# First input weights of layer 0 queued directly behind x in the same DMA queue

## The reference, cut to what matters

```python
h = x
for layer in range(DEPTH):
    z = rms_norm(h, norm_mix[layer]) @ w_in[layer]        # w_in: 1024 x 2072
    u_ssm, z_conv, q, k_c, v_c, ... = jnp.split(z, cuts, axis=-1)
    y_ssm = s5_mixer(u_ssm, ...)      # complex diagonal scan
    y_conv = conv_mixer(z_conv, ...)  # causal depthwise convolution
    y_nsa = nsa_mixer(q, k_c, ...)    # sparse attention
    h = h + concat(rms of the three) * mix_out_norm @ w_out
    h = h + cross_attention(rms_norm(h), rms_norm(mem), ...)
    h = h + (swiglu if layer is even else top-2-of-8 expert swiglu)(rms_norm(h))
```

## Time and profile before

| what | value |
|---|---|
| median of 3 runs | 1311.87 us (1309.08 to 1317.62) |
| the profiled execution's own time | 1314.63 us |
| span of the profiled execution | 1312.7 us |
| mean granted TensorE clock | 0.993 |
| PE busy | 1259.8 us, 96% of the span |
| DVE busy | 705.5 us, 54% |
| ACT busy | 428.7 us, 33% |
| DMA packets, bytes | 33980, 360.63 MB |

### The profile page before, as it was taken

One profiled execution on the slowest core, in us unless ns is written; L12 is line 12 of the kernel. 1 busy time (PEld: TensorE's weight loads), 2 busy tenths in 40 slices (PEclk: granted clock), 3 DMA queues, 4 the chain that ended last, 5 costly groups with the idle time before them and its releaser, 6 DMA issues.

```text
span 1312.7 us, 49682 instructions
## 1 busy us (share of the span) xinstructions
PE 1259.8 (96%) x21938; PEld 1070.7 (82%) x21938; DVE 705.5 (54%) x1640; ACT 428.7 (33%) x882; POOL 98.4 (7%) x157
## 2 busy tenths in 40 slices
PE   7999998999999999999889999999999999999897
PEld 5756566887887775656589999999999999999896
DVE  7875315647866376531455555555555554554455
ACT  4526313001002132631323333333333333333332
POOL 1360100000000044010000000000000000000010
PEclk9999999999999999999999999999999999999999
DMA  9530025233442543004779999999999999999994
GB/s 371 216 130 1 1 97 207 97 143 147 193 165 92 197 186 129 8 1 192 287 267 427 426 426 426 427 426 424 427 427 426 426 426 427 426 426 427 425 423 191
DMA packets 33980, 360.63 MB, mean 275 GB/s; under 512 B 3875, under 2 KB 5539, under 8 KB 7932
## 3 DMA queue, kind: packets, MB, share of 16 engines
q1 hardware_dynamic: 31184, 354.50, 65.4%
q10 hardware_dynamic: 2156, 3.19, 0.7%
q0 software_dynamic: 576, 2.10, 0.4%
HBM read 356.41 MB, written 3.36 MB: 274 GB/s over the span
## 4 chain that ended last, share of the span: by engine, by line
PE 79%; DMA 9%; DVE 7%; ACT 2%; issue 2%; POOL 0%; ACTq 0%; DVEq 0%; SPq 0%
PE bank L2317 25%; PE bank L1737 24%; PE bank L2334 12%; DMA ring<-moe_w_dram 8%; PE bank L2263 6%; PE bank L1745 2%; PE bank L2304 2%; PE bank L2024 1%; PE bank L1901 1%; PE bank L2111 1%; PE bank L1781 1%; PE bank L2089 1%; PE bank L2353 1%; PE bank L1840 1%; ACT ring L623 0%
## 5 line engine op out<-in xcount | busy, mean ns | idle before, releaser
L2317 PE MATMUL bank<-R,ring 128*64 128x80 f32 x11264 | 430.0, 233 | 15.2 <-DVE ring L1633 10.7
L2317 PEld LDWEIGHTS bank<-R,ring 128*64 128x64 f32 x11264 | 406.4, 137 | 23.7 <-DVE ring L1633 19.1
L1737 PE MATMUL bank<-ring 128*128 128x128 f32 (+2 forms) x1904 | 344.3, 340 | 5.0 <-DVE ring L1054 1.9
L1737 PEld LDWEIGHTS bank<-ring 128*128 128x128 f32 x1904 | 267.6, 192 | 84.9 <-issue 69.3
L899 ACT ACTIVATE ring<-ring 128x1024 f32<-128x1024 f32 x176 | 186.1, 1057 | 149.7 <-PE bank L2334 149.7
L2334 PE MATMUL bank<-zz,ring 128*64 128x80 f32 x5632 | 227.0, 234 | 0.0
L2334 PEld LDWEIGHTS bank<-zz,ring 128*64 128x64 f32 x5632 | 210.1, 138 | 0.0
L1633 DVE COPY ring<-ring 128x1024 f32<-128x1024 f32 x176 | 121.4, 690 | 37.3 <-DMA ring<-moe_w_dram 36.8
L1682 DVE SCALAR_TENSOR_TENSOR zz<-zz,bank 128x80 f32<-128x80 f32 x176 | 41.8, 238 | 158.3 <-PE bank L2317 157.2
L1637 DVE COPY ring<-ring 128x1024 f32<-128x1024 f32 x176 | 120.9, 687 | 0.1
L895 ACT ACTIVATE X<-bank 128x80 f32<-128x80 f32 x176 | 41.7, 237 | 233.5 <-PE bank L2317 232.6
(11 more groups left out here) (328 smaller groups left out, 1119.0 us busy)
## 6 DMA issues: line engine op xcount, KB each, us to landing
ring<-moe_w_dram SPq DMA_DIRECT2D x176, 1536.0 KB, 26.3
ring<-ffn_w_dram SPq DMA_DIRECT2D x11, 3072.0 KB, 10.3
ring<-w_in_dram SPq DMA_DIRECT2D x6, 2048.0 KB, 8.0
ring<-w_out_dram SPq DMA_DIRECT2D x4, 2048.0 KB, 7.8
ring<-w_x_dram SPq DMA_DIRECT2D x2, 3072.0 KB, 10.9
ring<-w_small_dram SPq DMA_DIRECT2D x2, 2896.0 KB, 11.3
ring<-w_in_dram SPq DMA_DIRECT2D x2, 2144.0 KB, 15.4
y_rows_dram<-R SPq DMA_DIRECT2D x7, 320.0 KB, 25.9
```

Of the source, the lines that this page charges most:

```text
L1737: i = pe.matmul(out_ap, a, b, start=(k == 0), stop=(k == n - 1))
L2317: e = pe.matmul(pb[out_bank][c0:c0 + 64, 0:CAP], half[:, P * k + c0:P * k + c0 + 64], xg[:, k], start=(k == 0), stop=(k == KT - 1), tile_p ...
```

## The change

SP no longer waits for x to land before it issues the first chunk of weights. The wait for `t5_loaded` that stands between this chunk and `mem` stays where it is, and no instruction of any other engine is changed. ACT's waits for `x_loaded` stay.

```diff
             for l in range(L):
-                if l == 0:
-                    sp.wait_ge(sem["x_loaded"], 16 * NT)
                 for c in (2, 3, 0, 1) if l else range(4):
                     item(f"in{c}_{l}", w_in[l][:, 4096 * c:4096 * c + (4288 if c == 3 else 4096)])
                     if l == 0 and c == 0:
```

## The result

The changed kernel took 1318.68 us (median of 20 runs, 1314.19 to 1323.64), the kernel before 1314.46 us in 20 runs beside it (1309.08 to 1318.42). The ratio is 1.0032, 95% interval 1.0019 to 1.0044: slower by 4.2 us, 2.5 to 5.8 by the interval.

The account below looks back on a forecast made before the run. The start was taken as bound by the chain from ACT's load of `par` through PE, ACT and DVE. +4.9 (`par`), 0 (weights) and 0 (`mem`) on the median 1311.87 gave 1316.8, said as 1317; range 1311 to 1322.

Parts of the forecast that it names:

- +4.9 us: whole kernel: sum of +4.9 from `par`, 0 for the weights, 0 for `mem`; bounds +4.3 and +4.9.
- The chain starts with `par`, not with the weights: kernel start: PE's work hangs on ACT's load of `par`; PE's 0.84 us wait for `in0_0` is worth nothing.
- One packet of each queue in turn: DMA engines: each takes one packet from q1 and q10 in turn, whatever their sizes, not sharing by bytes.
- The size of the toll, 4.3 to 4.9 us: ACT's queue at the start: 7 or 8 packets of `in0_0` per engine, 0.61 us each, pass ahead of `par`'s last.
- `tab` hidden by 1.9 us: bias table's load at the start: lands at 13.4, PE needs it at 15.3, so its delay costs nothing.
- `mem` at 13.4: SP's queue: `mem` issued at 13.4 after `tab`, lands at about 18, ACT wants it at 20.9: hidden.
- Nothing absorbs it: after 56.23: weight loads wait for slots PE frees and move with PE, so the 4.9 us delay stays.
- The clock, 0 taken and +2 kept for the range: PE's transposes: a later clock rise could double their time, at worst +2.0 us, at best nothing.
- The toll on the table alone: rival at the start: `par` on time, `tab` at 13.4, PE waits for it; +3.0 us, 1314.9; chance 0.08.
- No toll: rival at the start: ACT's loads held up by at most 1 us; time 1311 to 1312.5; chance 0.21.
- A rise of the clock so late that the change is slower by over 1%: rival in PE's projections: low clock level persists through them; 1325 us or more; chance 0.02.
- Whole blocks of 9 to 17 queued packets: DMA engines, skill's rule: `in0_0`'s eight rows could pass as one block; ahead of `par`, the same 4.9 us.

Follow-up runs that it names:

- before's second profile: the kernel before, unchanged, run once more for another profile: 1314.50 us, transposes 3.33 us, convolution at 58.04.

## Why the prediction was right

The forecast was 1317 us, the measurement 1318.68. The mechanism was right. In the number some luck is left: the sum stood on a median of three runs, 1311.87, where 20 runs gave 1314.46, so the same +4.9 us would have given 1319.4, and the ratio's +4.2 is a little under it.

- **The chain starts with `par`, not with the weights.** Right. PE's wait for `in0_0` went, and PE waited 1.8 us in place of 1.2 at the convolution; the weights brought nothing, and issuing them 0.5 us later (SP waiting for `par`) cost at most 0.2 us (convolution at 58.20 for 58.04).
- **One packet of each queue in turn.** Right: 71 against 73, and 166 against 169 with 4 KB rows, where the toll on `par` fell from 5.0 to 1.5 us.
- **The size of the toll, 4.3 to 4.9 us.** `par` moved from 7.49 to 12.47, by 4.98 us, all eight large rows and a little more.
- **`tab` hidden by 1.9 us.** Right: no wait in the change, and 1.88 us of it when 4.7 us more were put on it. **`mem` at 13.4.** It was 13.43, and it landed 5.0 us later, at 18.4 where I had put 18. `in0_0` landed at 12.3 (1.65 + 10.6) where I had put 11.8.
- **Nothing absorbs it.** Right: the convolution came 4.95 us later at like clock, and 507 us further on the distance of a like pair was still 5.1 us. Over the whole run the ratio gives 4.2 us (2.5 to 5.8) and the estimate at like clock 4.4 (3.6 to 5.1); both hold 4.9.
- **The clock, 0 taken and +2 kept for the range.** The first profile of the change showed nearly the whole +2, the second none. The bound was right, and that the late rise is no doing of the change is borne out by before's second profile. What I didn't weigh is that the profile of before that I read was itself on the favourable side by 2 us at the start; against an average execution of before the late rise is no cost of the change.
- **The rivals.** The toll on the table alone is out, since `par` was held up. No toll is out by the same row. A rise of the clock so late that the change is slower by over 1% is out by the ratio, 1.0032. Whole blocks of 9 to 17 queued packets, as the Trainium skill has it ("DMA: Bandwidth & Descriptors", "Queues, rings and completion order"), are not seen here: while the eight rows of `in0_0` went through, q10 moved 73 packets to q1's 71. That `par`'s toll fell with the size of a row tells packets from bytes, but not turns from blocks, since eight rows of 4 KB in one block would have cost about as little. Short blocks of two or three, of the same length in both queues, would give equal counts and the same toll and aren't told apart from single turns.

Left open: whether the rise of the clock comes late more often in one kernel than in the other; two profiles of each can't tell.

## What to carry to other kernels

A load that is issued earlier than needed isn't free when another queue still holds small rows that somebody waits for: here the eight 16 KB rows on each engine, 0.61 us each, delayed the 1 KB rows in the other queue by 4.98 us in all. Before taking away a wait ahead of a large load, list what the other queue still has to deliver, count per DMA engine its packets up to the load that somebody waits for and the large packets behind which they can fall, and multiply the smaller of the two counts by the time of one large packet. If the large load must be early, cut its rows small (1.5 us for 5.0 here), or leave only loads in the other queue that are needed late.

## What the runs showed of the hardware that was not expected

PE's clock did not rise at a fixed time after PE's start. With the same three fillers from nearly the same moment (7.49 and 7.36), one execution of the kernel before ran the transposes at 0.12 us each and another at 0.21. The rates are read as 2.4 GHz and mostly 1.2 GHz from the time of one matmul: in these first microseconds the clock column of the views says 1.00 even over the fillers, which take 0.49 us each where the same shape takes 0.23 later.

In the run with four loads ahead of x, `par` came 2.1 us earlier and PE idled for 3.1 us ahead of the transposes. The granted clock over the transposes was 0.50:

```profile
12.50:15.80 3.30, 3.04 (x15) 3.05 (x16) 1.56 (x4) 1.70 (x5) 0.80 (x2) 0.50 1.03 426
```

In the run with `cst` and `par` ahead of `s5_lam`, PE also idled for 3.1 us there, and the clock was 0.50 from 15.1 to 21.8 us. So in both executions the clock was at the low level after PE had idled for 3.1 us, though in the second the matmul ahead of the gap had run at the high rate (1.02 us for the bias table, against 1.87 in the slow starts).
